# Moving projection pieces in the weave of a decoder's first mixer: one within the last attention head, two within the sample group

## Chip, cores and metric

One NeuronCore of a Trainium2 chip. The metric is the device time of the program in microseconds (us); the median of three runs is given. TensorE is PE, ScalarE is ACT, VectorE is DVE, GpSimd is POOL, SyncE is SP.

## What is computed

The reference runs two trunk layers of a decoder for a prompt of 1024 tokens and for 8 samples of 4 tokens with 2048 tokens of cached past, all of width 1024. Only the first layer's mixer matters here:

```python
proj = u @ w_in                      # u: (tokens, 1024), w_in: (1024, 3072)
gate_b, gate_c, xin, q, k, v = jnp.split(proj, ...)        # six parts of 512 columns
conv_y, conv_new = short_conv(gate_c * xin, conv_w, conv_buf)   # width 3, per channel
y_conv = gate_b * conv_y
attn = diff_attend(q, k, v, mask, lam)    # 4 heads of 2 x 64; softmax 0 minus lam * softmax 1
attn = rmsnorm(attn, subln_g) * (1.0 - lam_init)
mixed = concatenate([y_conv, attn]) @ w_out
```

For the prompt the attention is causal over its own 1024 tokens; for a sample it runs over 16 pages of 128 cached keys and values, found through a page table, and its own 4 tokens. The feed-forward blocks, the second layer (mLSTM) and its states follow and are not touched.

## The kernel before

**Units and visits.** The projection is made transposed: a *visit* is one block of 128 weight columns (loaded as float32 by SP, split by ACT at L328 and DVE at L344 into a high and a low float16 part), and it has three *units*, one for each third (352) of the 1056 tokens. A unit is 24 matmuls of 128x352 (8 blocks of the contraction times 3 products of high and low parts, L371) into one PSUM bank. Visits 0 to 11 are q, k, v of the four heads. Visits 12 to 23 are the convolution's parts, three for each block of 128 channels: gate_c (copied out by ACT, L1490), xin (copied out and multiplied with gate_c by DVE, L1549, for the last third L1553 as well) and gate_b (DVE, L1568). Visit v has units 3v to 3v+2, so visit 14 has 42 to 44 and visit 20 has 60 to 62. Ahead of the first gate_b unit of a channel block DVE runs the convolution: two small copies (L1529, L1530) and the first tap (L1515, L1516) in the unit's first step, the second and third taps (L1518 to L1522) in its second step, ahead of the unit's copy. A gate_b unit is then cast to float16 by ACT (L1479, at the end L1495) in the next unit's first step, and its low part made by DVE (L1507) in the next unit's second step.

**Banks.** Units 36 to 44 alternate between PSUM banks 6 and 7; from unit 45 on all use bank 7, as bank 6 then collects the sample attention's output. The first half of a unit waits until the unit that last used its bank has been copied out:

```python
if ks[0] == 0:
    pe.wait_ge(w_ready, v + 1)
    if prev is not None:
        drained(pe, prev)
```

**The weave.** Attention work and projection work are two generators on each engine. `woven` (L899) advances the attention by one chunk and then the projection by as many steps as a list of counts says, again and again. On PE one step is half a unit (`pe_halves`, L2324: 12 matmuls, a *piece*); on ACT and DVE two steps make a unit, the first with the weight splits that are due at it, the second with the unit's copy out of PSUM. One and the same list is used on all engines, so the order is fixed on each queue. `HEAD_FILL` (L1576, 26 counts, 18 steps) serves each of the four heads; the last head's pieces are units 36 to 44. `SAMPLE_FILL` (L1844, 54 steps, units 45 to 71) serves the sample group, on SP too: there a step sequence of six is one visit, and the first of the six issues the weight load of the visit four further on (`sp_proj0`, L1878), between the page loads.

**A head's chunks** (`pe_head`, L1621; `act_head`, L1709; `dve_head`, L1790): an empty chunk, transposes of v, of k and of the samples' rows, two chunks for the tail of the head before. Then for each of 8 blocks of 128 queries: scores of the block after next or next (PE, L1604, L1607), row maxima (DVE, L1756), exponentials (ACT, L1696), the mix of the two softmaxes (DVE, L1763 to L1765); transposes of the mix (PE, L1669) in one chunk, or two from block 4 on; their copies out of PSUM (ACT, L1734; from block 4 on DVE also, L1825); and the value product (PE, L1683), a chunk of its own, with its copy and square by ACT (L1743, L1744).

**The sample group's chunks** (`pe_samples`, L1884; `act_samples`, L1976; `dve_samples`, L2021): first the last head's tail. DVE forms the square sums (L1772, L1773), ACT the root (L1702, behind a table load), DVE a Newton step (L681 to L684) and the scaling (L1781) and, behind these, small preparations; PE has nothing in this first chunk. Then two chunks, each a half of the tail: transposes (PE, L1618), copies by ACT (L1706) and DVE (L1787). Then two rounds of 4 samples each:

- 32 chunks of key pages: 8 transposes of two pages (PE, L1918), copies by ACT (L1987) and DVE (L2047), scores (PE, L1906); no projection steps.
- Four chunks: own scores (PE, L1925, L1929) with row maxima (DVE, L2042, L2054, L2055); exponentials (ACT, L1993, L1995, behind a table load) and then row sums and mixing weights (DVE, L2058 to L2061); weight transposition (PE, L1935, L1937); its second half (PE, L1942). On PE the second of these chunks is empty, and on ACT the first.
- 32 chunks of value pages (PE, L1957, L1964 at each sample's end), three chunks for root, scaling and transposition of the result (ACT, L2006 to L2016; DVE, L2073 to L2083; PE, L1972).

`load_page` (L1846) fetches pages into a ring of 16, half of them from SP and half from POOL; a page's load waits until PE has used the page 16 before.

Of the kernel before, what the change touches and what calls it, by code (L numbers as in the profile page):

```python
# [33 lines left out]
HEADS = 4  # L34
# [44 lines left out]
def build(nc, x_p, x_s, cache_k, cache_v, state_conv, state_C, state_n, state_m, page_table, norms, w_in0,  # L79
# [3 lines left out]
    with ctx:  # L83
# [815 lines left out]
        def woven(chunk, fill, between):  # L899

            for n in between:
                next(chunk)
                for _ in range(n):
                    next(fill)
            assert next(chunk, None) is None and next(fill, None) is None
# [562 lines left out]
        def act_proj0(act, v0, v1_):  # L1468

            later = None  # L1470
            for n in range(VISITS[v0].units[0], VISITS[v1_].units[-1] + 1):
                v, g, bank = UNITS[n].visit, UNITS[n].g, UNITS[n].bank
                h, m = v // 3, v % 3
                splits_hi(act, n)
                if later is not None:
                    drained(act, later)
                    if UNITS[later].visit == CXB + 5:
                        act.wait_ge(rows_saved, 32)
                    act.activation(mix[:, 0, UNITS[later].visit // 3 - HEADS, cols(UNITS[later].g)],  # L1479
                                   y_b[:, cols(UNITS[later].g)], ACT.Copy).then_inc(yb_hi, 1)  # L1480
                later = n if v >= CXB and m == 2 else None
                yield
                if v < CXB and m != 1:
                    act.wait_ge(unit_done, n + 1)
                    act.activation((qT if m == 0 else vT)[:, h, cols(g)], ps[:, bank, 0:GW], ACT.Copy,
                                   scale=(SCALE_DA if m == 0 else 1.0) / WS).then_inc(evac["act"], 1)
                if v >= CXB and m == 0:
                    act.wait_ge(unit_done, n + 1)
                    act.wait_ge(gate_c_used, h - HEADS)
                    act.activation(gate_c[:, cols(g)], ps[:, bank, 0:GW], ACT.Copy, scale=1 / WS).then_inc(  # L1490
                        evac["act"], 1)
                yield
            if later is not None:
                drained(act, later)
                act.activation(mix[:, 0, UNITS[later].visit // 3 - HEADS, cols(UNITS[later].g)],  # L1495
                               y_b[:, cols(UNITS[later].g)], ACT.Copy).then_inc(yb_hi, 1)
# [77 lines left out]
                low(later)  # L1574

        HEAD_FILL = (0,) + (1,) * 5 + (1, 0) * 3 + (1, 1) + (1, 1, 0) * 4  # L1576

        def group_at(i, part_):

# [260 lines left out]
            ins.then_inc(q_ready, 1)  # L1840


        ROUND_FILL = ((0,) * 32 + (2, 2, 2, 2) + (1, 0) * 15 + (0, 0) + (1, 1, 1))
        SAMPLE_FILL = (1, 1, 0) + ROUND_FILL * 2  # L1844

        def load_page(eng, f):  # L1846

# [1065 lines left out]
        @block.scalar  # L2913
        def _(act):
            chain = Chain(act, act_c)
            for tt in range(1, NTT, 2):
                act.dma_start(arena[0:P, tt, 0:D], x_p[0, tt * P:(tt + 1) * P, :]).then_inc(x_loaded[tt], 16)
            act.wait_ge(lam_ready, 1)
            act.activation(roots[:, 1, 0:1], roots[:, 0, 0:1], ACT.Abs_reciprocal_sqrt)
            for tt in range(NTT):  # L2920
                w = P if tt < NTT - 1 else TS
                act.wait_ge(x_loaded[tt], 16)
                if tt >= 2:
                    act.wait_ge(sq_ready, tt - 1)
                ins = act.activation(sq[tt % 2][0:w, 0:D], arena[0:w, tt, 0:D], ACT.Square,
                                     accum_out=roots[0:w, 3, tt:tt + 1])
                if tt:
                    ins.then_inc(sq_ready, 1)
                if tt == AHEAD:
                    act_first_root(act, 0, AHEAD)  # L2930
            act_first_root(act, AHEAD, NTT)
            split_hi(act, 0)
            split_hi(act, 1)
            act_first_norm(act)
            act.wait_ge(lam_ready, 2)
            act.activation(lam_e, lam_e, ACT.Exp).then_inc(misc_ev, 1)
            for _ in act_proj0(act, 0, 2):
                pass
            for h in range(HEADS):
                woven(act_head(act, h), act_proj0(act, 3 * h + 3, 3 * h + 5), HEAD_FILL)  # L2940
            woven(act_samples(act), act_proj0(act, CXB + 3, WO0 - 1), SAMPLE_FILL)
            act_boundary(act, 0, act_ffn(act, WAVE[0]))
            for _ in act_ffn(act, FFU[0][12:]):
                pass
            act_boundary(act, 1, act_first_heads(act))
            act_mlstm(act, chain)
            act_short_boundary(act, act_ffn(act, WAVE[2]))
            for _ in act_ffn(act, FFU[1][12:]):
                pass
            act_end(act)  # L2950

        @block.vector
        def _(dve):
            chain = Chain(dve, dve_c)
            dve_links["t"] = chain
            chain.link(dve.memset(roots[:, :, :], 1.0))
            chain.link(dve.memset(eps_col[:, :], D * EPS))
            dve.sem_inc(lam_ready, 1)
            for tt in range(NTT):
                w = P if tt < NTT - 1 else TS  # L2960
                dve.wait_ge(x_t, tt + 1)
                dve.tensor_copy(hT[:, :, tt * P:tt * P + w], flat(2 * (tt % 2), 1024).rearrange(
                    "p (k t) -> p k t", t=P)[:, :, 0:w]).then_inc(x_ev, 1)
            first_diagonals(dve, chain, AHEAD, NTT)
            dve.wait_ge(misc_t, 1)
            t = ps[:, 7, :]
            dve.tensor_scalar(gains[:, 0:8], t[:, 0:8], math.sqrt(D), None, ALU.mult)
            dve.tensor_scalar(gains[:, 8:64], t[:, 8:64], -0.5 * math.sqrt(D), None, ALU.mult)
            dve.tensor_scalar(gains[:, GM:GM + 8], t[:, 64:72], math.sqrt(MLD), None, ALU.mult)
            dve.tensor_scalar(gains[:, GS:GS + 1], t[:, 72:73], math.sqrt(P) * (1 - LAM_INIT), None, ALU.mult)  # L2970
            dve.tensor_copy(gains[:, GC:GC + 12], t[:, 73:85])
            dve.tensor_copy(nT[:, :, :, :].rearrange("p b h k -> p (b h k)"), t[:, 128:192])
            chain.link(dve.tensor_copy(stT[:, :, :].rearrange("p k n -> p (k n)"), t[:, 256:320]))
            dve.wait_ge(x_ev, NTT)
            split_lo(dve, 0)
            dve_first_norm(dve, chain)
            dve.wait_ge(lam_loaded, 16)
            l4 = lam_rows.rearrange("p (f d) -> p f d", f=4)
            chain.link(dve.tensor_tensor(lam_prod.rearrange("p (f d) -> p f d", f=2), l4[:, 0:4:2, :], l4[:, 1:4:2, :],
                                         ALU.mult))  # L2980
            dve.tensor_reduce(lam_e, lam_prod.rearrange("p (f d) -> p f d", f=2), AX.X, ALU.add).then_inc(lam_ready, 1)
            dve.wait_ge(misc_ev, 1)
            chain.link(dve.scalar_tensor_tensor(neg_lam, lam_e[:, 1:2], -LAM_INIT, lam_e[:, 0:1], ALU.add,
                                                ALU.subtract))
            for _ in dve_proj0(dve, chain, 0, 2):
                pass
            for h in range(HEADS):
                woven(dve_head(dve, chain, h), dve_proj0(dve, chain, 3 * h + 3, 3 * h + 5), HEAD_FILL)
            woven(dve_samples(dve, chain), dve_proj0(dve, chain, CXB + 3, WO0 - 1), SAMPLE_FILL)
            dve.wait_ge(misc_t, 2)  # L2990
            dve.wait_ge(kv_stored, 32 * HEADS)
            dve.tensor_copy(conv_nat[:, :], ps[0:2 + 2 * NB, 7, :]).then_inc(conv_ev, 1)
            dve_boundary(dve, chain, 0, dve_ffn(dve, WAVE[0]))
            for _ in dve_ffn(dve, FFU[0][12:]):
                pass
            dve_boundary(dve, chain, 1, dve_first_heads(dve))
            dve_mlstm(dve, chain)
            dve_short_boundary(dve, chain, dve_ffn(dve, WAVE[2]))
            for _ in dve_ffn(dve, FFU[1][12:]):
                pass  # L3000
            dve_end(dve, chain)

        @block.tensor
        def _(pe):
# [24 lines left out]
                unit(pe, n, u)  # L3029
            pe.wait_ge(const_ready, 3)  # L3030
            for h in range(HEADS):
                woven(pe_head(pe, h), pe_halves(pe, range(9 * h + 9, 9 * h + 18), u), HEAD_FILL)
            woven(pe_samples(pe), pe_halves(pe, range(3 * CXB + 9, 3 * WO0), u), SAMPLE_FILL)
            pe.wait_ge(mix_ready, 3 * HC)
            drained(pe, last_unit(WO0 - 1))
# [42 lines left out]
```

## Time and profile before

| | us |
|---|---|
| median of 3 runs | 2736.68 (2736.4 to 2737.29) |
| the profiled execution | 2740.7 |
| its span in the profile | 2739.1 |
| PE busy in the span | 2631.2 (96%) |
| DVE busy | 1248.0 (46%) |
| ACT busy | 1023.4 (37%) |
| GpSimd busy | 451.0 (16%) |
| mean granted clock of TensorE | 0.987 of full speed |

The span is the time from the first to the last recorded instruction of that execution. PE's matmuls are pipelined: the time printed for a group runs from its first start to its last end, so the groups overlap by a little. Idle time in brackets is what stood ahead of a group, with the engine and line that released it; "issue" there means that the profile shows no wait. In the timeline the four heads run from 62 to 318 us, the sample group from 318 to 585 us: first keys at 329 to 383, first values at 403 to 450, second keys at 457 to 509, second values at 530 to 576.

### The profile page before, as it was taken

Reading aid. Unit: us, or ns where it says so; the run is one execution under the profiler, and the core shown is the slowest. Engines: PE = TensorE matmul, PEld = TensorE weight load, DVE = VectorE, ACT = ScalarE, POOL = GpSimd, SP = SyncE. Lnnn points to the kernel's source line nnn. Section 1 sums busy time; section 2 is a strip of 40 time slices with the busy share of each in tenths; the row PEclk is TensorE's granted clock in tenths of the full one; section 3 lists DMA queues with packets and bytes.
Section 4 is the critical chain, followed back from the end, with each engine's and each line's share of the span. In section 5 each row is a group of like instructions: output and inputs, shape, how many; then the busy total and the mean of one; then the engine's idle time right before and its main releaser. Section 6 shows DMA issues by size and latency. Waiting matters only on the chain.

```text
span 2739.1 us, 49474 instructions
## 1 busy us (share of the span) xinstructions
PE 2631.2 (96%) x20215; PEld 1877.7 (69%) x20215; DVE 1248.0 (46%) x2064; ACT 1023.4 (37%) x1886; POOL 451.0 (16%) x512
## 2 busy tenths in 40 slices
PE   8999899999999999999999999999989999999997
PEld 5666566655688668876567666667647886788764
DVE  5555533336744214545663433344467441244444
ACT  4454432224444213433433232324355341234332
POOL 4000023222122002212201010110101210122121
PEclk9999999999999999999999999999999999999998
DMA  7111269761211311134435332332411121111542
GB/s 248 60 39 41 68 228 346 241 239 53 73 63 43 87 35 62 63 122 119 105 79 79 60 84 66 78 82 66 163 52 67 63 59 58 37 58 47 153 117 85
DMA packets 257516, 266.15 MB, mean 97 GB/s; under 512 B 10652, under 2 KB 217794, under 8 KB 256652
## 3 DMA queue, kind: packets, MB, share of 16 engines
q1 hardware_dynamic: 231772, 166.10, 21.9%
q0 software_dynamic: 24944, 94.79, 9.7%
q8 instruction: 162, 2.65, 0.4%
q10 hardware_dynamic: 576, 2.10, 0.2%
q14 instruction: 62, 0.51, 0.1%
HBM read 227.45 MB, written 35.50 MB: 96 GB/s over the span
## 4 chain that ended last, share of the span: by engine, by line
PE 89%; DVE 5%; ACT 2%; issue 2%; DMA 1%; POOL 0%; DVEq 0%; SPq 0%; ACTq 0%; POOLq 0%
PE ps L371 48%; PE ps L1114 24%; PE ps L1918 2%; PE ps L1604 1%; PE ps L1906 1%; PE ps L1683 1%; PE ps L1957 1%; PE ps L2457 1%; PE ps L2437 1%; PE ps L2471 1%; DVE arena L872 1%; DVE w_split L344 1%; DVE hT L876 1%; PE ps L2494 1%; PE ps L2481 1%
## 5 line engine op out<-in xcount | busy, mean ns | idle before, releaser
L371 PE MATMUL ps<-u,w_split 128*128 128x352 f16 (+1 forms) x4752 | 752.0, 315 | 9.6 <-DVE u L736 5.9
L371 PEld LDWEIGHTS ps<-u,w_split 128*128 128x128 f16 (+1 forms) x4752 | 462.5, 98 | 260.0 <-issue 20.4
L371 PE MATMUL ps<-arena,w_split 128*128 128x352 f16 x3663 | 559.9, 313 | 4.1 <-DVE w_split L344 1.5
L371 PEld LDWEIGHTS ps<-arena,w_split 128*128 128x128 f16 x3663 | 357.5, 98 | 200.7 <-issue 9.4
L1114 PE MATMUL ps<-hT,w_split 128*128 128x264 f16 x3456 | 400.6, 276 | 3.2 <-ACT arena L1154 3.2
L1114 PEld LDWEIGHTS ps<-hT,w_split 128*128 128x128 f16 x3456 | 337.8, 98 | 54.9 <-issue 2.1
L344 DVE SCALAR_TENSOR_TENSOR w_split<-w_raw,w_split 128x1024 f16<-128x1024 f32 (+2 forms) x133 | 184.6, 1389 | 309.9 <-ACT w_split L328 309.3
L1114 PE MATMUL ps<-u,w_split 128*128 128x264 f16 x2592 | 303.4, 276 | 0.0
L1114 PEld LDWEIGHTS ps<-u,w_split 128*128 128x128 f16 x2592 | 253.6, 98 | 38.3
L328 ACT ACTIVATE w_split<-w_raw 128x1024 f16<-128x1024 f32 (+2 forms) x133 | 155.6, 1172 | 149.3 <-PE ps L371 101.0
L342 DVE SCALAR_TENSOR_TENSOR w_split<-arena,w_split 128x512 f16<-128x512 f32 x126 | 85.9, 724 | 103.9 <-ACT w_split L322 103.9
L1244 POOL TENSOR_TENSOR arena<-arena 128x512 f32<-128x512 f32 x18 | 22.8, 1266 | 527.0 <-DVE w_split L342 527.0
L342 DVE SCALAR_TENSOR_TENSOR w_split<-w_raw,w_split 128x512 f16<-128x512 f32 x126 | 80.9, 687 | 62.4 <-ACT w_split L322 62.4
L371 PE MATMUL ps<-arena 128*128 128x352 f16 x657 | 105.4, 321 | 0.0
L810 POOL TENSOR_TENSOR arena<-arena 128x352 f32<-128x352 f32 x54 | 75.7, 1402 | 174.4 <-ACT arena L798 174.2
L2304 ACT ACTIVATE arena<-ps 128x352 f32<-128x352 f32 x66 | 30.5, 464 | 179.4 <-PE ps L371 179.3
L1187 DVE TENSOR_TENSOR arena<-ps,arena 128x528 f32<-128x528 f32 x36 | 25.5, 708 | 153.3 <-ACT arena L1154 153.3
L1284 ACT ACTIVATE arena<-ps 128x352 f32<-128x352 f32 x48 | 22.3, 465 | 191.3 <-PE ps L371 191.3
L371 PEld LDWEIGHTS ps<-arena 128*128 128x128 f16 x657 | 65.7, 100 | 39.3 <-issue 2.4
L1200 DVE TENSOR_TENSOR arena<-arena 128x1056 f16<-128x1056 f32 (+1 forms) x60 | 58.3, 972 | 50.4 <-ACT arena L1137 41.4
L371 PE MATMUL ps<-u,arena 128*128 128x352 f16 x504 | 77.5, 313 | 3.2 <-ACT arena L1282 2.7
L322 ACT ACTIVATE w_split<-arena 128x512 f16<-128x512 f32 x126 | 71.8, 620 | 13.7 <-PE ps L1114 10.9
(398 smaller groups left out, 2988.5 us busy)
## 6 DMA issues: line engine op xcount, KB each, us to landing
w_raw<-in_w_down SPq DMA_DIRECT2D x58, 704.0 KB, 4.9
w_raw<-in_w_in SPq DMA_DIRECT2D x56, 512.0 KB, 8.3
arena<-in_w_gu SPq DMA_DIRECT2D x18, 1024.0 KB, 5.2
w_raw<-in_w_gu SPq DMA_DIRECT2D x18, 1024.0 KB, 5.2
hT<-in_cache_k SPq DMA_DIRECT2D x64, 256.0 KB, 4.3
hT<-in_cache_k POOLq DMA_DIRECT2D x64, 256.0 KB, 4.5
hT<-in_cache_v SPq DMA_DIRECT2D x64, 256.0 KB, 5.0
hT<-in_cache_v POOLq DMA_DIRECT2D x64, 256.0 KB, 5.4
```

The source lines that it names most:

```text
L322: act.activation(split_of(v, 0).rearrange("p (k n) -> p k n", k=kt), raw_of(v), ACT.Copy, scale=WS).then_inc(w_hi, 1)
L328: act.activation(split_of(v, 0)[:, 0:kt * n], raw_of(v), ACT.Copy, scale=WS).then_inc(w_hi, 1)
L342: dve.scalar_tensor_tensor(lo, raw_of(v), WS, hi, ALU.mult, ALU.subtract).then_inc(w_ready, 1)
L344: dve.scalar_tensor_tensor(split_of(v, 1)[:, 0:kt * n], raw_of(v), WS, split_of(v, 0)[:, 0:kt * n], ALU.mult, ALU.subtract).then_inc(w_rea ...
L371: ins = pe.matmul(ps[0:m, bank, 0:GW], split_of(v, wp)[:, k * w + col * P:k * w + col * P + m], x[:, xp, k0 + k, cols(g)], start=(k == 0 a ...
L810: pool.tensor_tensor(sum_y, sum_y, sq_y[k % 2], ALU.add).then_inc(y_added, 1)
L872: ins = dve.scalar_tensor_tensor(h_tmp[:, k % 2, :], ybuf[:, k, cols(g)], gains[:, col:col + 1], rs[0], ALU.mult, ALU.mult)
L876: dve.tensor_tensor(h, h, h_tmp, ALU.add).then_inc(h_ready, 1)
L1114: ins = pe.matmul(ps[:, bank + s_, 0:HW], split_of(v, wp)[:, k * P:(k + 1) * P], x, start=(name in ("M1", "M2", "M5") and k == 0 and q == ...
L1200: dve.tensor_tensor(hi_lo[:, 1], x, hi_lo[:, 0], ALU.subtract).then_inc(hid_ready, 1)
L1918: ins = pe.transpose(ps[:, 4 + e, h * P:(h + 1) * P], ring[:, f % RING, h * P:(h + 1) * P], ident[:, :])
L2304: act.activation((q_of[h % 2], k1, v1, o1)[m // 2][:, m % 2, cols(g)], ps[:, UNITS[n].bank, 0:GW], ACT.Sigmoid if m >= 6 else ACT.Copy, sc ...
```

## The change

Three lists of counts. In the last head a list `LAST_FILL` takes the place of `HEAD_FILL`: the piece behind the transposes of block 2 is left out there, and two pieces instead of one stand behind the first transposes of block 7. In the sample group three steps instead of one stand ahead of the tail's first half, and in each round's value pages there are 14 steps instead of 15, the last four chunks having none. The sums stay 18 and 54.

```diff
--- before.py
+++ after.py
@@ -1574,6 +1574,7 @@
                 low(later)
 
         HEAD_FILL = (0,) + (1,) * 5 + (1, 0) * 3 + (1, 1) + (1, 1, 0) * 4
+        LAST_FILL = (0,) + (1,) * 5 + (1, 0) * 2 + (0, 0) + (1, 1) + (1, 1, 0) * 2 + (1, 1, 0) + (2, 1, 0)
 
         def group_at(i, part_):
 
@@ -1840,8 +1841,8 @@
             ins.then_inc(q_ready, 1)
 
 
-        ROUND_FILL = ((0,) * 32 + (2, 2, 2, 2) + (1, 0) * 15 + (0, 0) + (1, 1, 1))
-        SAMPLE_FILL = (1, 1, 0) + ROUND_FILL * 2
+        ROUND_FILL = ((0,) * 32 + (2, 2, 2, 2) + (1, 0) * 14 + (0,) * 4 + (1, 1, 1))
+        SAMPLE_FILL = (3, 1, 0) + ROUND_FILL * 2
 
         def load_page(eng, f):
 
@@ -2937,7 +2938,7 @@
             for _ in act_proj0(act, 0, 2):
                 pass
             for h in range(HEADS):
-                woven(act_head(act, h), act_proj0(act, 3 * h + 3, 3 * h + 5), HEAD_FILL)
+                woven(act_head(act, h), act_proj0(act, 3 * h + 3, 3 * h + 5), HEAD_FILL if h < HEADS - 1 else LAST_FILL)
             woven(act_samples(act), act_proj0(act, CXB + 3, WO0 - 1), SAMPLE_FILL)
             act_boundary(act, 0, act_ffn(act, WAVE[0]))
             for _ in act_ffn(act, FFU[0][12:]):
@@ -2985,7 +2986,7 @@
             for _ in dve_proj0(dve, chain, 0, 2):
                 pass
             for h in range(HEADS):
-                woven(dve_head(dve, chain, h), dve_proj0(dve, chain, 3 * h + 3, 3 * h + 5), HEAD_FILL)
+                woven(dve_head(dve, chain, h), dve_proj0(dve, chain, 3 * h + 3, 3 * h + 5), HEAD_FILL if h < HEADS - 1 else LAST_FILL)
             woven(dve_samples(dve, chain), dve_proj0(dve, chain, CXB + 3, WO0 - 1), SAMPLE_FILL)
             dve.wait_ge(misc_t, 2)
             dve.wait_ge(kv_stored, 32 * HEADS)
@@ -3029,7 +3030,7 @@
                 unit(pe, n, u)
             pe.wait_ge(const_ready, 3)
             for h in range(HEADS):
-                woven(pe_head(pe, h), pe_halves(pe, range(9 * h + 9, 9 * h + 18), u), HEAD_FILL)
+                woven(pe_head(pe, h), pe_halves(pe, range(9 * h + 9, 9 * h + 18), u), HEAD_FILL if h < HEADS - 1 else LAST_FILL)
             woven(pe_samples(pe), pe_halves(pe, range(3 * CXB + 9, 3 * WO0), u), SAMPLE_FILL)
             pe.wait_ge(mix_ready, 3 * HC)
             drained(pe, last_unit(WO0 - 1))
```

## Rows read from the trace of the kernel before

**Rows 1.** The page's chain that ended last, by engine.

```profile
PE 89%; DVE 5%; ACT 2%; issue 2%; DMA 1%; POOL 0%; DVEq 0%; SPq 0%; ACTq 0%; POOLq 0%
```

**Rows 2.** PE timeline, head 3: start us, us, instruction, [idle before <-releaser].

```profile
274.86 1.95 PE L371 MATMUL ps<-u,w_split 128*128 128x352 f16 x12
...
276.80 0.94 PE L1683 MATMUL ps<-arena 128*128 128x128 f32 x6
...
299.95 1.72 PE L1683 MATMUL ps<-arena 128*128 128x128 f32 x12 [2.68 <-issue]
...
301.60 3.49 PE L1604 MATMUL ps<-arena 64*128 64x512 f32 x8
```

**Rows 3.** PE timeline, head 0, block 5 and the scores behind it.

```profile
105.68 1.58 PE L1683 MATMUL ps<-arena 128*128 128x128 f32 x12 [1.60 <-issue]
...
107.19 1.99 PE L1604 MATMUL ps<-arena 64*128 64x512 f32 x8
```

**Rows 4.** Stretches: busy PE, PEld, DVE, ACT, POOL; granted clock, DMA share.

```profile
300.00:304.00 4.00, 4.00 (x18) 2.56 (x20) 3.86 (x8) 0.54 (x3) 0.00 (x0) 0.66 0.39 115
...
328.00:332.00 4.00, 2.96 (x13) 2.46 (x14) 1.42 (x2) 0.60 (x1) 0.00 (x0) 0.57 0.39 96
```

**Rows 5.** PE timeline, end of head 3 to the first page transposes.

```profile
318.25 1.95 PE L371 MATMUL ps<-u,w_split 128*128 128x352 f16 x12
...
323.09 0.66 PE L1618 MATMUL ps<-ident,arena 128*128 128x128 f32 x4 [2.88 <-DVE arena L1781]
...
326.59 0.63 PE L1618 MATMUL ps<-ident,arena 128*128 128x128 f32 x4 [1.06 <-DVE arena L1787]
...
329.04 3.49 PE L1918 MATMUL ps<-ident,hT 128*128 128x128 f32 x16 [1.82 <-issue]
```

**Rows 6.** Timeline of round one, all engines, and round two's first transposes.

```profile
387.16 1.28 ACT L1993 ACT_TABLE_LOAD   x1
...
391.55 0.16 DVE L2058 TENSOR_REDUCE small<-small 128x1 f32<-128x5 f32 x1 [8.17 <-ACT arena L1995]
...
409.03 1.06 PE L1957 MATMUL ps<-hT,arena 128*4 128x128 f32 x32
...
415.54 0.53 DVE L1568 SCALAR_TENSOR_TENSOR arena<-ps,arena 128x352 f32<-128x352 f32 x1
...
456.79 1.04 PE L1918 MATMUL ps<-ident,hT 128*128 128x128 f32 x8
```

**Rows 7.** Waits of 335 to 600 us: who waited for whom, us, times, longest.

```profile
POOL hT L1853 <- PE ps L1957: 79.9, 27, 25.0
```

**Rows 8.** Timeline of round two, all engines, 509 to 530 us.

```profile
509.70 3.75 PE L371 MATMUL ps<-u,w_split 128*128 128x352 f16 x24
...
513.55 1.06 ACT L328 ACTIVATE w_split<-w_raw 128x1024 f16<-128x1024 f32 x1 [0.27 <-PE ps L371]
...
514.11 0.16 DVE L2058 TENSOR_REDUCE small<-small 128x1 f32<-128x5 f32 x1
...
514.22 3.74 PE L371 MATMUL ps<-u,w_split 128*128 128x352 f16 x24 [0.78 <-DVE arena L1553]
...
517.08 1.28 DVE L1518 SCALAR_TENSOR_TENSOR arena<-arena,gains 128x1024 f32<-128x1024 f32 x1
...
520.72 3.74 PE L371 MATMUL ps<-u,w_split 128*128 128x352 f16 x24 [0.59 <-DVE arena L1568]
...
529.70 0.62 PE L1957 MATMUL ps<-hT,arena 128*4 128x128 f32 x16
```

**Rows 9.** ACT and DVE timelines, head 3, blocks 2, 5 and 6.

```profile
276.25 0.50 ACT L1734 ACTIVATE arena<-ps 128x384 f32<-128x384 f32 x1
...
299.77 1.28 DVE L1518 SCALAR_TENSOR_TENSOR arena<-arena,gains 128x1024 f32<-128x1024 f32 x1
...
302.72 0.52 DVE L1568 SCALAR_TENSOR_TENSOR arena<-ps,arena 128x352 f32<-128x352 f32 x1
...
305.29 2.36 DVE L1756 TENSOR_REDUCE small<-ps 128x1 f32<-128x1024 f32 x2 [0.53 <-PE ps L1607]
```

## Prediction

> **What bounds the kernel now.** I read the page first: the chain that ended last is 89% TensorE [rows 1], so time moves only where TensorE (PE) stands still or runs at its lower clock. The change touches 250 to 585 us. There I read the timelines of PE, ScalarE (ACT) and VectorE (DVE) side by side, and looked at every idle stretch of PE.
>
> Four things are to be seen. (1) In the last head PE waits 2.68 us ahead of the value product of block 5 [rows 2]; in each of the three heads before it waits 1.60 at that place (the first of them is shown, [rows 3]). The granted clock then falls to 0.66 on the mean of 4 us, that is partly at 1.2 GHz [rows 4], and eight score matmuls take 3.49 instead of 1.99 [rows 2, 3]. (2) Between the last head and the sample group PE waits 2.88, 1.06 and 1.82 us, and the clock falls again (0.57), so that 16 transposes take 3.49 where eight take 1.04 in the second round [rows 4, 5, 6]. (3) In the value phases GpSimd's page queue waits for PE (79.9 us in all), PE does not wait for pages [rows 7]: a piece taken out there gives its time back. (4) At the head of each round's value phase stand eight pieces in four pairs. In the second round a pair is one whole unit (first half, second half), and all these units share PSUM bank 7: a unit's first half waits until the unit before it has been copied out.
>
> **The change part by part.** A "piece" is half a projection unit, 12 matmuls; 59a and 59b are the halves of unit 59. 24 of these matmuls take 3.74 us and 12 take 1.95 [rows 2, 8], so one more piece costs 1.8 us of PE. No instruction is added and the units keep their order; pieces only move against the attention work. The count of pieces ahead of each point changes its parity, and that decides what follows.
>
> *Last head, block 2: a piece leaves.* Behind it stands the value product at 276.80, released by ACT's copy at 276.25 (0.50 long) [rows 2, 9]; the piece before it runs 274.86 to 276.65. Without it PE waits 1.8 us for the same copy and starts the product at the same time. Gain 0.
>
> *Last head, blocks 3 to 7: one piece less is done at each point, two at the end.* In block 5 DVE's weight split and first conv tap (visit 14, unit 42) now come behind the probability copy instead of ahead of it: the 2.68 wait and its clock loss go. The two other taps with the unit's copy, 3.4 us from 299.77 to 303.2 [rows 9], move into block 6, between the row maxima (2.36 us [rows 9]) and that block's probability copy. Worked through: value product 5 at 297.1 (no wait), scores, then 0.4 of waiting for DVE's mix, maxima until 303.4, taps and unit copy until 306.8, copy until 307.4. PE has done its two pieces by 305.4 and waits 2.0 us; value product 6 starts at 307.45 instead of 309.49. Then a piece more than before: product 7 at 315.45 instead of 316.47. **-1.0 us.** The 2.0 us wait is new, and nothing in the trace shows whether it lowers the clock: a wait of 1.60 did not, one of 2.68 did [rows 2, 3]. Bounds 0 and 1.7 (1.5 on the scores, 0.15 on the product [rows 2, 3]); it lies nearly half way, I take 0.8. The wait of 1.8 in block 2 has the same two bounds; being near 1.60, I take 0.
>
> *Front of the sample group: three pieces instead of one before the tail's transposes.* These wait for a chain ACT, DVE, ACT, DVE (square sums, root, Newton, scaling) that ends 4.84 us after the start of the first piece (318.25 to 323.09 [rows 5]). Three pieces are 5.4; the third is a new unit's first half and waits for ACT's copy of bank 7, some 0.6 (a DVE one is 0.59 to 0.78 [rows 8]). The transposes come 6.0 after the first piece, 1.2 later than now. The fourth piece lies between the tail's halves as before. The end is set by ACT's and DVE's copy of the second half, which then come 1.0 sooner against PE's work: page transposes at 10.6 after the first piece, 10.8 now. **-0.2 us** with two more pieces done. The waits are now 0.6 and 1.6, apart, so the second fall of the clock goes too: 3.49 against twice 1.04 is 1.4, of which the waits for the copies between the pages hide some: **-1.0** (bounds 0, -1.4).
>
> *Value phases: one piece fewer in each.* A pair's period less two short page products is 1.9; nothing else fills it: **-3.8 us.** If pages were late this would be 0; SyncE's weight load moves with its step and waits at most for a split that comes earlier too, and both page queues run 16 pages ahead, so neither delays PE. GpSimd's order has no pieces in it.
>
> *First round, four pairs.* They hold units 47 to 50 instead of 46 to 49; the first pair is still whole, so exponentials keep their place. Unit 49's first half waits 0.15 for unit 48. Unit 51, with its split and taps, now begins with the first value pages: from unit 50's last matmul to unit 51's copy took 7.0 us (409.03 to 416.07 [rows 6]), while PE's own work up to unit 52 is 6.6 now: 0.5. **+0.8 us** with two smaller waits for unit 50's copy and in the round's end.
>
> *Second round, four pairs: the expensive place.* The pairs are now second half, first half: 59b 60a, 60b 61a, 61b 62a, 62b 63a. Two consequences. On ACT, the weight split that belongs to unit 60's first half stood behind the exponentials (513.55 [rows 8]); now it stands ahead of them and waits for unit 59's end. 59b ends at 511.5, split until 512.8, and only then the table load and the exponentials, since the load stands right ahead of the first exponential, as in round one where it followed the unit's copy. From the load to DVE's first sum took 4.4 us (387.16 to 391.55 [rows 6]): 517.2. Four small DVE instructions, an estimated 0.8 (the first is 0.16 [rows 8]), then taps two and three and unit 60's copy: 517.08 to 520.72, 3.6 [rows 8]. So bank 7 is free at 521.6. On PE, 61a stands directly behind 60b, and ahead of the weight transposition that so far covered that chain. PE: 59b until 511.5, 0.9 for bank 7, 60a 60b until 516.0, then idle **5.6 us** until 521.6. From there: what took 11.9 us until the first value page (517.8 to 529.70 [rows 8]), less 0.6 of its wait, plus one piece 1.8, plus two bank waits of 0.8 in the turned pairs: 14.7. Value pages start at 536.2 instead of 529.70: **+6.5 us.** And a wait that long lowers the clock, since 2.68 did: +1.5 (bounds 0 and 3.2, for one fall or two). The wait of 0.2 ahead of unit 63 goes: -0.2.
>
> The Trainium skill (ScalarE: Activation LUTs, What ACT_TABLE_LOAD costs) gives a set switch a drain of some 1.4 us besides the load of about 1.28. The trace has the 1.28, and the exponential follows it at once in its timeline, so no drain is paid visibly here; by the page's figure the second round would cost 1.4 more.
>
> **Sum:** -1.0 + 0.8 - 0.2 - 1.0 - 3.8 + 0.8 + 6.5 + 1.5 - 0.2 = +3.4 us. The profiled execution took 2740.7 us for a span of 2739.1; the median of the runs shown is 2736.68, 4 us lower, and I add the sum to that: **2740.1 us**. About 0.2% (5.5 us) is what a measurement of this kernel can tell from no change; this lies within it.
>
> **The rivals.** *The clock falls everywhere (ends slower).* If a wait of about 1.8 to 2.0 is enough, the clock falls in block 2 and at value product 6, and the 5.6 us wait brings two low stretches: +1.5, +0.9 and +1.5 more, 2744.0. For it: 2.68 did it. Against: 1.60 did not, in three heads, and part of a slow stretch would be spent waiting for DVE anyway. It decides from the wait length between the two. Chance 0.15.
>
> *The second round does not stall.* If the exponentials still came first, or unit 60's copy were ready, the turned pairs would cost four bank waits of 0.8 in place of 0.8 and 0.6, +1.7 instead of 8.0: about 2733.8. Against it: the order of both queues is fixed by the same list of counts. Chance 0.08.
>
> *Value phases are held by the pages.* Then the two pieces give nothing back: 2743.9. For it only the DMA's load there; against it that PE is the one waited for [rows 7]. Chance 0.02.
>
> **How the numbers follow.** My forecast holds with 0.75; its own range, by its clock bounds, is 2737 to 2743, and a little of it lies above 2742.2. The range of 2735.5 to 2743.5 leaves out most of the clock rival and of the one without a stall. Faster by over 0.2%: even without the stall the gain is 3, so 0.03. Slower by over 0.2%: the clock and page rivals and the upper end of my own case, 0.18. Within: 0.79.
>
> **What would show it.** Right: PE's timeline has no wait before value product 5, one of about 2 us before product 6 and 1.8 before product 2; three pieces and no wait over 1 us before the tail's transposes; and in round two, ahead of the weight transposition, one wait of 5 to 6 us for DVE's L1568, with ACT's table load behind L328. Wrong: that wait absent or under 2 us, or page waits on PE in the value phases.

## The result and the profile after

The changed kernel took 2743.53 us (median of 12 runs, 2740.72 to 2749.67) against 2737.37 for the kernel before (12 runs, 2733.71 to 2742.92): ratio 1.0026, 95% interval 1.0016 to 1.0036. It is slower by 0.26%, outside the range of the prediction by a hair and on the far side of its bound of 0.2%. The profiled executions, however, took 2740.72 and 2740.7 us, with the same span of 2739.1. So the times of one program scatter by more than the effect, and the traces have to be compared by stretches.

From here on "the stretch" is what the change touches: from the last head's transposes of block 0 (L1669; one line further down in the new file) to the transposes of the conv rows (L3037). In the PE timeline before it went from 268.67 to 584.93, 316.26 us:

```profile
268.67 0.28 PE L1669 MATMUL ps<-ident,arena 128*128 128x128 f32 x1
...
584.93 0.61 PE L3037 MATMUL ps<-ident,conv_new 128*18 128x128 f32 x4 [1.77 <-DVE arena L1507]
```

After:

```profile
268.04 0.28 PE L1670 MATMUL ps<-ident,arena 128*128 128x128 f32 x1
...
587.92 0.60 PE L3038 MATMUL ps<-ident,conv_new 128*18 128x128 f32 x4 [1.78 <-DVE arena L1507]
```

That is 319.88 us, **+3.6**. The last head and the end of it, where rows 2 and 5 show the kernel before:

```profile
276.17 0.94 PE L1684 MATMUL ps<-arena 128*128 128x128 f32 x6 [1.77 <-ACT arena L1735]
...
296.48 1.50 PE L1684 MATMUL ps<-arena 128*128 128x128 f32 x12
...
297.91 1.99 PE L1605 MATMUL ps<-arena 64*128 64x512 f32 x8
...
300.46 0.66 PE L1670 MATMUL ps<-ident,arena 128*128 128x128 f32 x4 [0.34 <-DVE arena L1766]
...
306.63 1.80 PE L1684 MATMUL ps<-arena 128*128 128x128 f32 x14 [1.61 <-issue]
...
314.53 1.95 PE L1684 MATMUL ps<-arena 128*128 128x128 f32 x16
...
320.70 1.95 PE L371 MATMUL ps<-u,w_split 128*128 128x352 f16 x12 [0.65 <-ACT arena L1490]
...
322.49 0.60 PE L1619 MATMUL ps<-ident,arena 128*128 128x128 f32 x4
...
327.20 1.06 PE L1919 MATMUL ps<-ident,hT 128*128 128x128 f32 x8 [1.83 <-issue]
```

Value product 5 (296.48) stands without a wait, its scores take 1.99. The waits moved to product 2 (1.77, for ACT's copy) and product 6 (1.61). Three pieces stand ahead of the tail's transposes (322.49), the third after 0.65 for ACT's copy of bank 7; eight page transposes take 1.06 and not 3.49 for sixteen. In round two ACT had its table load and its exponentials ahead of the split in the kernel before:

```profile
507.35 1.28 ACT L1993 ACT_TABLE_LOAD   x1
...
510.22 0.69 ACT L1993 ACTIVATE arena<-ps,small 128x512 f32<-128x512 f32 x1 [1.59 <-DVE small L2055]
```

The same place in the changed kernel, all engines (compare rows 8):

```profile
506.28 1.96 PE L371 MATMUL ps<-u,w_split 128*128 128x352 f16 x12
...
508.34 1.06 ACT L328 ACTIVATE w_split<-w_raw 128x1024 f16<-128x1024 f32 x1 [4.43 <-PE ps L371]
...
509.01 3.74 PE L371 MATMUL ps<-u,w_split 128*128 128x352 f16 x24 [0.77 <-DVE arena L1553]
...
509.41 1.28 ACT L1994 ACT_TABLE_LOAD   x1
...
509.50 1.23 DVE L344 SCALAR_TENSOR_TENSOR w_split<-w_raw,w_split 128x1024 f16<-128x1024 f32 x1 [0.63 <-ACT w_split L328]
...
513.86 0.16 DVE L2059 TENSOR_REDUCE small<-small 128x1 f32<-128x5 f32 x1 [2.18 <-ACT arena L1996]
...
514.62 1.28 DVE L1518 SCALAR_TENSOR_TENSOR arena<-arena,gains 128x1024 f32<-128x1024 f32 x1
...
517.57 0.52 DVE L1568 SCALAR_TENSOR_TENSOR arena<-ps,arena 128x352 f32<-128x352 f32 x1
...
518.24 3.68 PE L371 MATMUL ps<-u,w_split 128*128 128x352 f16 x12 [5.49 <-DVE arena L1568]
...
521.85 0.18 PEld L1936 LDWEIGHTS ps<-arena 128*32 128x32 f32 x2 [0.57 <-issue]
...
534.84 0.62 PE L1958 MATMUL ps<-hT,arena 128*4 128x128 f32 x16
```

On ACT the split (508.34) and behind it the table load (509.41) now stand ahead of the exponentials; DVE's row sum comes at 513.86, its taps behind it, unit 60's copy at 517.57; and PE stands idle for 5.49 us ahead of 61a. That piece then takes 3.68 us instead of 1.95. The granted clock there, columns as in rows 4:

```profile
300.00:304.00 4.00, 3.66 (x28) 2.64 (x27) 4.00 (x5) 2.79 (x5) 0.00 (x0) 1.00 0.27 80
...
328.00:332.00 4.00, 3.66 (x36) 2.18 (x35) 1.99 (x3) 1.66 (x3) 1.13 (x2) 1.00 0.67 175
...
516.00:520.00 4.00, 1.76 (x7) 0.91 (x8) 2.03 (x4) 0.50 (x1) 0.00 (x0) 0.50 0.00 0
...
520.00:524.00 4.00, 4.00 (x24) 2.67 (x23) 0.64 (x2) 0.00 (x0) 0.00 (x0) 0.70 0.00 0
```

The two falls of rows 4 are gone (1.00 and 1.00). One longer fall has come: 0.50 over 516 to 520 and 0.70 over the next four, that is 1.2 GHz for some seven microseconds, part of them spent idle.

Taken apart at the same instructions on PE, before against after, beside the prediction (us):

| part | before | after | difference | predicted |
|---|---|---|---|---|
| block 0 to value product 7 | 47.80 | 46.49 | -1.31 | -1.0 and 0.8 for a fall |
| to the first page transposes | 12.57 | 12.67 | +0.10 | -0.2 |
| first keys to the first pair | 53.85 | 52.93 | -0.92 | -1.0 |
| first pairs and values | 73.90 | 73.25 | -0.65 | +0.8 - 1.9 |
| second keys | 52.91 | 52.90 | 0.0 | 0 |
| second pairs (509.70 to 529.70; 506.28 to 534.84) | 20.00 | 28.56 | +8.56 | +6.5 + 1.5 |
| second values to the conv rows | 55.23 | 53.08 | -2.15 | -1.9 - 0.2 |
| sum | 316.26 | 319.88 | +3.62 | +3.4 |

Each part came within 0.6 us, the head but for the fall that I had half expected. These are two single profiles, and the experiments show that their falls of the clock belong to the execution as much as to the program. What is left to explain is why the medians differ by 6.2 when this stretch differs by 3.6 in the profiles.

### The profile page after: what moved, and what is told of

It reads as the page before. It is cut to its first block, busy times and chain, and to the rows that moved or that the text cites. A ratio compares the mean times of both kernels' runs of the same rounds, so it can differ in the third digit from the quotient of the medians.

```text
span 2739.1 us, 49475 instructions
## 1 busy us (share of the span) xinstructions
PE 2628.5 (96%) x20215; PEld 1875.7 (68%) x20215; DVE 1247.9 (46%) x2064; ACT 1022.9 (37%) x1886; POOL 450.1 (16%) x512
## 4 chain that ended last, share of the span: by engine, by line
PE 87%; DVE 5%; ACT 3%; issue 2%; DMA 1%; POOL 0%; DVEq 0%; SPq 0%; POOLq 0%; ACTq 0%
PE ps L371 47%; PE ps L1114 24%; PE ps L1919 2%; PE ps L1907 1%; PE ps L1605 1%; PE ps L1684 1%; PE ps L2458 1%; PE ps L1958 1%; PE ps L2438 1%; PE ps L2472 1%; DVE arena L872 1%; DVE hT L876 1%; DVE w_split L344 1%; PE ps L2495 1%; PE ps L2482 1%
```

## The experiments

The diffs are against the changed kernel unless said otherwise. Every kernel was timed over five rounds beside the kernel before, except the last four, which are single profiles. Two theories went in. **A:** the turned pairs of round two cost more than everything else gains, and what exceeds that is the clock falling at places that the change does not touch. **B:** the new waits in the last head lower the clock and make the loss.

### The changed kernel again

No edit.

> The changed kernel once more, for a second profile and more times. Stretch: from the last head's first block transpose (L1669, here L1670) to the conv transposes (L3037, here L3038), 316.3 us before and 319.9 in the profile after. Theory A (second round): the stretch is again 319 to 321, with the 5.5 us wait for DVE's L1568 in it, and the rest of the measured difference (6 us in the medians, 3.6 in the stretch) comes from clock falls at places that the change does not touch, so it differs from run to run. Theory B (clock in the last head): the stretch is 321 to 324 in this profile, with a fall of the clock at the 1.8 us or 1.6 us wait that the first profile did not have.

Measured: 2740.73 (11 runs, 2739.51 to 2741.86) against 2736.61, ratio 1.0013 (1.0003 to 1.0022); stretch 320.05, with the wait of 5.49. Another sample of the same program gives +4.1 us where the first gave +6.2.

### The last head's list alone

```diff
-        ROUND_FILL = ((0,) * 32 + (2, 2, 2, 2) + (1, 0) * 14 + (0,) * 4 + (1, 1, 1))
-        SAMPLE_FILL = (3, 1, 0) + ROUND_FILL * 2
+        ROUND_FILL = ((0,) * 32 + (2, 2, 2, 2) + (1, 0) * 15 + (0, 0) + (1, 1, 1))
+        SAMPLE_FILL = (1, 1, 0) + ROUND_FILL * 2
```

> Only the last head's list is changed, the sample group keeps its old list. Theory A: the 2.68 us wait of block 5 goes and one of 1.6 and one of 1.8 stand elsewhere; stretch 315 (1 less than before), time 1 less or equal, ratio 0.9995. Theory B: falls at these waits make it 1 to 3 us slower than before.

Measured: 2736.38 (11 runs), ratio 0.9997 (0.9988 to 1.0006). No loss, against B; and no gain that can be told. Its profile is of its slowest execution (2744.89), so it does not stand for the median, but it shows what can eat the gain: the same wait ahead of product 2 (1.78), but here the clock falls behind it, and again in round one's pairs. Stretch 320.03.

```profile
276.00:280.00 4.00, 2.70 (x12) 1.57 (x14) 2.27 (x4) 1.78 (x8) 0.00 (x0) 0.80 0.25 60
...
394.00:402.00 8.00, 8.00 (x37) 5.38 (x37) 1.31 (x2) 1.54 (x2) 0.00 (x0) 0.57 0.15 44
```

### The sample group's lists alone

```diff
-                woven(..., HEAD_FILL if h < HEADS - 1 else LAST_FILL)
+                woven(..., HEAD_FILL)
```

> Only the sample group's lists are changed, the last head keeps its old list. Theory A: stretch 321 (4.6 more than before), time 4 to 6 us more, ratio 1.0018. Theory B: 2 us or less more.

Measured: 2742.59 (8 runs), ratio 1.0024 (1.0013 to 1.0035): 6 us more than before, the whole loss. The stretch is 328.44 in its profile (of its slowest execution, 2748.19), 7.4 over the 321 expected. Some 5 us of that lie behind the wait:

```profile
521.85 3.68 PE L371 MATMUL ps<-u,w_split 128*128 128x352 f16 x12 [5.49 <-DVE arena L1568]
...
525.80 3.68 PE L1938 MATMUL ps<-arena 128*128 128x64 f32 x16
...
529.27 3.73 PE L371 MATMUL ps<-u,w_split 128*128 128x352 f16 x12
...
533.71 3.63 PE L371 MATMUL ps<-u,w_split 128*128 128x352 f16 x12 [0.71 <-DVE arena L1568]
...
538.90 1.95 PE L371 MATMUL ps<-u,w_split 128*128 128x352 f16 x12
```

```profile
300.00:304.00 4.00, 3.71 (x22) 2.22 (x22) 3.86 (x8) 0.53 (x3) 0.00 (x0) 1.00 0.42 123
...
516.00:540.00 24.00, 17.80 (x81) 11.33 (x79) 6.12 (x14) 2.95 (x9) 0.00 (x0) 0.64 0.06 18
```

The wait is the same 5.49, but the clock stays low: 0.64 on the mean of 24 us is 17 us at 1.2 GHz, and the three pieces and the weight transposition take 3.6 to 3.7 where they take 1.95 and 2.00 at full clock. From the start of 61a to the first value page it is 21.60 us here and 16.21 to 16.91 in seven profiles of the changed kernel; in the run with the split put off (below), where the clock stays full, it is 14.66. So the clock's price behind that wait is 1.6 to 2.3 us in those seven and 6.9 here. Another 1.7 us of the stretch is a fall in round one's pairs (first pair to first value page 22.28 instead of 20.60), a place that the change leaves alone. The first row says something else too: here the old 2.68 wait of block 5 stands ahead of 300 us and the clock is 1.00.

### The pairs of round two alone

The kernel before, with the last piece of round two's first value phase put into round one's instead, so that only round two's pairs are turned:

```diff
-        SAMPLE_FILL = (1, 1, 0) + ROUND_FILL * 2
+        FIRST_ROUND = (0,) * 32 + (2, 2, 2, 2) + (1, 0) * 16 + (1, 1, 1)
+        SECOND_ROUND = (0,) * 32 + (2, 2, 2, 2) + (1, 0) * 14 + (0,) * 4 + (1, 1, 1)
+        SAMPLE_FILL = (1, 1, 0) + FIRST_ROUND + SECOND_ROUND
```

> The kernel before, with one piece moved from the second round's value pages to the end of the first round's value pages: the front and the last head stay, only the pairs at the head of round two are turned (59b 60a, 60b 61a, ...). Theory A: the 5.5 us wait stands there, the pairs cost 6.5 and the clock 1.5 to 2; nothing is gained elsewhere, ratio 1.0030, 8 us more. Rival (the turned pairs are not what costs): 2 us or less more.

Measured: 2744.96 (6 runs), ratio 1.0031 (1.0019 to 1.0043), 8.4 us more; stretch 324.99.

```profile
523.97 3.68 PE L371 MATMUL ps<-u,w_split 128*128 128x352 f16 x12 [5.49 <-DVE arena L1568]
```

From the first pair of round two to the first value page it is 28.91 us against 20.00 before. One piece moved from one value phase to the other, nothing else, and the loss is there in full. The cause is shown.

### Why the wait is so long: the split put off

The changed kernel, with the weight split due at unit 60 made due at unit 61:

```diff
             late[WO0 + i] = PASS[0][0][i - 2]
+        late[CXB + 10] = 61
```

> The changed kernel with one thing put off: the weight split that stood at unit 60's first half (ScalarE L328, VectorE L344) stands at unit 61's, behind the exponentials; the pairs stay turned. Theory A, in which the long wait is made by the split and the table load ahead of the exponentials: the table load comes back ahead of unit 59's end, the exponentials start some 3.9 us earlier, and the wait for L1568 shrinks from 5.5 to about 2.3 us, with a fall of the clock less often: 3 to 5 us less than the changed kernel, within 1 us of the kernel before. Rival A2 (the wait is the two convolution taps alone): it stays 5 us and the time stays at 4 us over before.

Measured: 2735.38 (11 runs), ratio 0.9994 (0.9985 to 1.0003): 1.2 less than before, which cannot be told from nothing, and against before 5 to 8 less than the three samples of the changed kernel; stretch 313.97. In its timeline the table load stands at 503.76, ahead of the pairs, as it did before the change:

```profile
503.76 1.28 ACT L1995 ACT_TABLE_LOAD   x1
...
506.63 0.69 ACT L1995 ACTIVATE arena<-ps,small 128x512 f32<-128x512 f32 x1 [1.59 <-DVE small L2057]
...
509.82 0.16 DVE L2060 TENSOR_REDUCE small<-small 128x1 f32<-128x5 f32 x1
...
513.53 0.52 DVE L1569 SCALAR_TENSOR_TENSOR arena<-ps,arena 128x352 f32<-128x352 f32 x1
...
514.21 1.95 PE L371 MATMUL ps<-u,w_split 128*128 128x352 f16 x12 [1.62 <-DVE arena L1569]
```

The exponentials start 3.9 us earlier against the first piece than in the changed kernel (0.5 behind 506.11, 4.4 behind 506.28), and the wait is 1.62 (2.3 expected). The rival A2, that the taps alone make the wait, falls: of the 5.5 us, 3.9 are made by the order on ACT, and DVE's row sums, taps and copy leave the rest. DVE's part of the split moved too, but it was not what held PE: in the changed kernel DVE stood 2.18 us waiting for ACT behind it (513.86 above).

### Whole units at the head of round two

```diff
-        SAMPLE_FILL = (3, 1, 0) + ROUND_FILL * 2
+        SECOND_ROUND = (0,) * 32 + (1, 2, 2, 2) + (1, 0) * 15 + (0, 0) + (1, 1, 1)
+        SAMPLE_FILL = (3, 1, 0) + ROUND_FILL + SECOND_ROUND
```

> The changed kernel with second round counts (1, 2, 2, 2) and then 15 single pieces again: one half and then whole units stand at the head of round two. Theory A: no 5.5 us wait, one of 2.6 ahead of unit 61 instead, that round costs what it did before; 5 to 7 us less than the changed kernel, 1 to 3 us less than before, ratio 0.9990. Rival (the loss is not in the pairs): no more than 1 us off the changed kernel.

Measured: 2735.12 (11 runs), ratio 0.9990 (0.9981 to 0.9999), stretch 314.96 with a fall in it, at product 2. The wait ahead of unit 61 is 1.79, not the 2.6 expected:

```profile
519.83 3.74 PE L371 MATMUL ps<-u,w_split 128*128 128x352 f16 x24 [1.79 <-DVE arena L1568]
```

This is the only version whose interval lies below one: 1.4 us under the kernel before in the medians, and so within the bound of 0.2% that the prediction took as what a measurement can tell from nothing.

### Both front pieces from round one, with the new and the old list of the last head

```diff
-        SAMPLE_FILL = (3, 1, 0) + ROUND_FILL * 2
+        FIRST_ROUND = (0,) * 32 + (2, 2, 2, 2) + (1, 0) * 13 + (0,) * 6 + (1, 1, 1)
+        SECOND_ROUND = (0,) * 32 + (2, 2, 2, 2) + (1, 0) * 15 + (0, 0) + (1, 1, 1)
+        SAMPLE_FILL = (3, 1, 0) + FIRST_ROUND + SECOND_ROUND
```

> The changed kernel with both front pieces taken out of the first round's value pages (13 single pieces, then six chunks without), round two exactly as before. Theory A: the pairs of round two are whole units, front and last head keep their gain: about 4.5 us less than before (-1.0 head, -0.2 and -1.0 front, -3.8 for the two pieces, +0.8 round one, up to +0.7 for pages that come late at the end of the first value phase), ratio 0.9983. Rival (front pieces give nothing back): no change from before.

> As the run before this one, with the last head's list as it was before. Theory A: 3.5 us less than before, 1 us more than with the last head's new list. Rival (clock falls at the last head's new waits outweigh its gain): faster than with the last head's new list.

Measured: 2737.26 and 2736.16 (11 runs each), ratios 0.9995 (0.9985 to 1.0006) and 0.9995 (0.9986 to 1.0004). Both miss the -4.5 and -3.5, and they cannot be told apart. The waits of PE in the first of them show a part of it:

```profile
PE ps L1960 <- DMA hT<-in_cache_v: 1.8, 2, 1.1
```

With two pieces fewer in the first value phase, pages come late by 1.8 us in all (2.1 with the old head), nearly what one piece takes. From the first value page of round one to round two's first transposes it is 52.24 and 52.93 us, against 52.04 to 53.22 in the seven profiles of the changed kernel with one piece out: the second piece gives back next to nothing. The rest is in part the clock: the first has falls at product 2 and in round one's pairs, stretch 316.37, the second at block 5 and in round one's pairs, 316.72.

### The kernel before again

No edit.

> The kernel before, unchanged, for a second profile: where the clock falls in it. Theory A (falls depend on how a wait lies in time, not on the wait alone): the waits of 2.68 in block 5 and of 2.88, 1.06 and 1.82 behind the last head are there to 0.05 us, while the falls beside them may be there or not; stretch (from the last head's first block transpose to the conv transposes) 314 to 319 us. Rival (each of these waits always brings its fall): both falls again, stretch 316.3 within 0.3.

Measured: 2736.97 (11 runs), ratio to the same kernel 1.0003 (0.9994 to 1.0013), stretch 315.28. Its waits are those of rows 2 and 5 to 0.05 us, its clock is not:

```profile
300.59 1.58 PE L1683 MATMUL ps<-arena 128*128 128x128 f32 x12 [2.69 <-issue]
...
323.41 1.11 PE L1618 MATMUL ps<-ident,arena 128*128 128x128 f32 x4 [2.88 <-DVE arena L1781]
...
329.62 1.06 PE L1918 MATMUL ps<-ident,hT 128*128 128x128 f32 x8 [1.86 <-issue]
```

```profile
300.00:304.00 4.00, 3.41 (x20) 2.10 (x20) 3.86 (x9) 0.53 (x3) 0.00 (x0) 1.00 0.46 131
```

The wait of 2.69 ahead of product 5, and no fall (product 1.58, clock 1.00). The tail's transposes at 323.41 take 1.11 instead of 0.66: the other fall came earlier, and there it cost less. From product 7 to the first pair it is 65.76 us here and 66.42 in the first profile; without a fall there, in all fourteen profiles with the new front, it is 65.6.

### The changed kernel a third time, and both cures together

> The changed kernel a third time, for a third profile and more times. Theory A: the 5.5 us wait ahead of unit 61 again, stretch 319.5 to 322 or, where the low clock behind that wait holds on as it did in the run with the sample group alone, 325 to 329. Times in the range 2739.5 to 2750, in one or two heaps.

Measured: 2742.72 (11 runs, 2737.43 to 2748.51), ratio 1.0027 (1.0016 to 1.0037), stretch 320.22.

```diff
-        SAMPLE_FILL = (3, 1, 0) + ROUND_FILL * 2
+        SECOND_ROUND = (0,) * 32 + (1, 2, 2, 2) + (1, 0) * 15 + (0, 0) + (1, 1, 1)
+        SAMPLE_FILL = (3, 1, 0) + ROUND_FILL + SECOND_ROUND
...
+        late[CXB + 10] = 61
```

> Both cures together: counts (1, 2, 2, 2) and 15 single pieces in round two, and the split of unit 60 put off to unit 61. Theory A: VectorE's chain to unit 60's copy is shorter by its split of 1.2, so the 1.79 us wait ahead of unit 61 falls to about 0.6: 1.2 less than with the whole pairs alone, ratio to before 0.9985.

> As the run before this one, with the last head's list as it was before. Theory A: 1 us more than that (the last head's new list gains 1.0), that is no difference that this measurement can tell; the 2.68 us wait is back in block 5.

Measured: 2734.30 and 2733.31 (11 runs each), ratios 0.9995 (0.9986 to 1.0004) and 0.9993 (0.9984 to 1.0002). The wait ahead of unit 61 is 0.52 in both, as expected; whether the medians are 1.5 and 2.5 us better than before, these runs can't tell. The stretch is 315.10 in the first, with falls at product 2 and in round one's pairs, and 312.66 in the second, the shortest of all, with none.

### Four single profiles of the changed kernel

> Changed kernel, one profile. Theory A: if its time is 2747.5 us or more, the low clock behind the 5.5 us wait lasts some 17 us and the matmuls up to the first value page run at half speed (a piece 3.7 us), stretch 326 to 329; if it is 2744 or less, the low clock there lasts 7 us and the stretch is 319.5 to 322. Rival: a time in the upper heap with a stretch of 322 or less, the falls being elsewhere.

> As e13: time 2747.5 or more goes with a stretch of 326 to 329 (theory A), or with 322 or less (rival).

> As e13: time 2747.5 or more goes with a stretch of 326 to 329 (theory A), or with 322 or less (rival).

> As e13: time 2747.5 or more goes with a stretch of 326 to 329 (theory A), or with 322 or less (rival).

Measured, time and stretch: 2742.58 and 321.82; 2740.30 and 319.56; 2746.61 and 320.07; 2742.01 and 323.72. None reached 2747.5, so the test as stated did not come about; the last one missed what was expected of a time under 2744 (a stretch of 319.5 to 322). But the slowest of them has a short stretch, and the longest stretch a middling time: what lies outside (time less stretch) was 2417.2 to 2426.5 us over seven profiles of one program. The two longer stretches have a fall behind product 2 that the others lack, here in the first of the four, whose second row has the shortest fall behind the 5.49 us wait:

```profile
280.00:284.00 4.00, 4.00 (x24) 2.69 (x22) 1.66 (x5) 2.15 (x5) 0.00 (x0) 0.66 0.33 99
...
516.00:532.00 16.00, 9.80 (x59) 6.17 (x58) 5.23 (x12) 3.02 (x9) 0.00 (x0) 0.89 0.09 26
```

The longest stretch, 323.72, has one more fall, in round one's pairs, behind a wait of 1.41 us that stands there in all eighteen profiles; 24 matmuls take 5.42 instead of 3.74:

```profile
392.31 0.30 PE L1936 MATMUL ps<-arena 128*32 128x64 f32 x2 [1.41 <-DVE arena L2062]
...
394.38 5.42 PE L371 MATMUL ps<-u,w_split 128*128 128x352 f16 x24
```

### What the granted clock of every run says

No run was added for this. Most timed runs come with their span and their mean granted clock (those of the kernel before in the first comparison do not). Their product is an estimate of the span without the low clock; the clock is given to 0.001, 2.7 us of the span, so only means over many runs count. The three samples of the changed kernel have means of 2705.7, 2705.5 and 2706.0 us, the three sets of the kernel before that were timed with the experiments (25, 33 and 33 runs) 2701.6, 2701.4 and 2701.2. So some 4.3 us of the loss are there whatever the clock does, in every sample within half a microsecond, and what the three comparisons differ by is in the main the clock. The eight longest runs of the changed kernel (2747.8 us and more, of 34) have a mean clock of 0.9855, the other 26 one of 0.9875: on a span of 2743 that is 5.5 of the 7.1 us between their means. Where in the kernel these eight ran at the low clock is not on record.

## Why the prediction was wrong

The mechanism was right, and so was its place; what failed is the price of the clock, and with it a small term for pages. *Last head:* the 2.68 wait went, products 2 and 6 took 1.77 and 1.61 (1.8 and 2.0 worked out), product 7 came 1.3 earlier against block 0 (1.0). *Front:* three pieces and 0.65 of waiting, page transposes 12.67 after product 7 against 12.57; the two more pieces were done for nothing, as worked out, but the 0.2 on top did not come. *Round one:* 0.52 ahead of unit 52 (0.5). *Round two, pairs:* a wait of 5.49 (5.6), for L1568, with the split and the table load ahead of the exponentials, and the value pages 8.56 later against the first pair (8.0). The first exponential starts at 510.71, 0.02 behind the end of the table load, so no drain shows there, where the figure of the Trainium skill (ScalarE: Activation LUTs, What ACT_TABLE_LOAD costs) would have given 1.4 more. By the two first profiles the sum was +3.62 against +3.4. That agreement is luck: the profile before had two falls of the clock, worth 0.3 and up to 0.8 us, and the one after had neither the fall at product 2 nor any late page to speak of.

Set against the means of all profiles of the two kernels, seven after and two before, the sum comes to +5.0 (us):

| part | predicted | measured |
|---|---|---|
| block 0 to value product 7 | -0.2 | -0.69 |
| to the first pair | -0.2 - 1.0 | -0.49 |
| first pairs and values | +0.8 - 1.9 | -0.35 |
| second keys | 0 | 0.0 |
| second pairs | +6.5 + 1.5 | +8.62 |
| second values to the conv rows | -1.9 - 0.2 | -2.09 |
| sum | +3.4 | +4.99 |

The step that failed, term by term:

- *The fall behind the last head, booked as a gain of 1.0, with 0.2 for the earlier transposes.* I took what one profile of the kernel before showed for part of that kernel. The fall does stand in all four profiles with the old front and in none of the fourteen with the new, but its cost hangs on where it comes: from product 7 to the first pair the old front took 65.76, 65.93, 66.42 and 66.55 us, the new one 65.6. Both gains together are 0.2 to 0.95, not 1.2.
- *The clock behind the 5.49 us wait, 1.5.* It cost 2.0 on the mean of seven profiles (16.65 us from 61a to the first value page, against 14.66 at full clock), and 6.9 in the run with the sample group alone.
- *The last head, where the sum came out by luck.* I put 0 on the 1.8 wait ahead of product 2 and 0.8 on the one ahead of product 6. The clock fell at product 2 in 6 of 12 profiles with the new list and cost 1.6 us each time (block 0 to product 7: 48.1 instead of 46.49); it never fell at product 6. The fall in block 5, which the list removes, stands in two of six profiles with the old list (before, and the front alone) and costs 0.3 (47.80 against 47.48). So the new list gains 1.0 where no clock falls and 0.3 on the mean of all profiles, near the 0.2 booked, for other reasons.
- *Pages and the clock in round one, 0.* In six of the seven profiles PE waits 0.2 to 1.0 us for value pages of round one, 0.5 on the mean, and one of the seven has the fall in round one's pairs, 1.7.

The rival of the clock named product 2 and the long wait rightly, but made it a question of wait length, which the waits of 1.41 and 1.60 us refute (last section).

The medians, then. The stretch gives +5.0 on the mean; the three timed comparisons gave +6.2, +4.1 and +7.0 us. By the estimate from the granted clocks 4.3 us are there at any clock and the rest is the clock, and it differs from sample to sample. A low clock of 17 us behind the wait, as seen once with the sample group alone in a run of 2748.19, would bring 5 us more, much of what parts the eight longest runs from the others; none of the seven profiles caught it, but none of them was of such a run. Falls outside the stretch would do as well: that stays open. The base was low too: the three runs that I built on have a median of 2736.68, the twelve 2737.37. And the range was too narrow: its top, 2743.5, took the clock's bounds one at a time and gave no room to the scatter between two sets of runs.

The two rivals that I thought unlikely fell: round two does stall (undone by whole units, the loss goes), and value pages are not held by pages, but for the 0.2 to 1.0 us above and the second piece taken from one round.

## What to carry to other kernels

When pieces of filler work are moved between slots of a fixed order, write out which half of which unit lands in every slot behind the move: a shift by one half turned first and second halves around, put a copy's consumer directly behind its producer, and on another engine put a blocking instruction and a table load ahead of the softmax. Shift by whole units, or repair the count at the next group. Before a clock fall beside a wait is booked as cost or gain, look whether it is there, and what it costs, in several profiles of the same program. Where two comparisons of the same programs disagree, multiply each run's span with its mean granted clock: what is left of the difference stands at full clock too, within the rounding of the clock.

## What the runs showed of the hardware that was not expected

The same wait, at the same place to 0.05 us, brings the granted clock down in one execution and not in the next: 2.68 us in block 5 in 2 of 6 profiles, 1.77 ahead of product 2 in 6 of 12. The Trainium skill (TensorE: Matmul & The Clock Gate, Part 1: The HAM clock gate) says that the number of matmuls at the low clock at a kernel's start differs from run to run of the same kernel; these profiles show such scatter in the middle of a kernel. The length of the wait does not order it: the 1.60 in block 5 of the first three heads never brought a fall (54 waits of 1.59 or 1.60 in eighteen profiles), nor did the 1.61 ahead of product 6 (12), while the shorter 1.41 in round one's pairs brought one in 6 of 18. What else stands around these waits was not varied, so why they differ is open. Once down behind the 5.5 us wait, the clock was low for 3.5 us in one execution (0.89 over 16 us), for about 7 in most, and for 17 in one whose work behind the wait was the same.
